# A two-layer decoder step on eight cores: planner waits taken from a table by pair of engines, and up to three seven-product sets open at once

## What is computed

```python
for i in range(DEPTH):                                      # 2 layers
    a = rmsnorm(h, norm_mix[i])
    proj = jnp.einsum('btd,de->bte', a, w_in[i])            # 1024 -> 2048: u, B, C, v
    ...
    y_pool, pb = pool_mixer(u, pool_bufs[i], start, pool_w[i], pool_scale[i])
    z, cb = short_conv(cg * v, conv_bufs[i], conv_w[i], conv_b[i])
    mix = jnp.concatenate([y_pool, bg * z], axis=-1)
    h = h + jnp.einsum('btm,md->btd', mix, w_out[i])
    m = rmsnorm(h, norm_mlp[i])
    f = jax.nn.relu(jnp.einsum('btd,df->btf', m, w_up[i]))  # 1024 -> 4096
    h = h + jnp.einsum('btf,fd->btd', f * f, w_down[i])     # 4096 -> 1024
    gate = jax.nn.sigmoid(jnp.einsum('btd,de->bte', rmsnorm(h, norm_ple[i]), w_ple_gate[i]))
    h = h + gate * jnp.einsum('btq,qd->btd', p[i], w_ple_proj[i])
    ...
return rmsnorm(h, norm_f), ...
```

## Time and profile before

| | us |
|---|---|
| median of 3 runs | 1455.05 (1454.87 to 1456.32) |
| the profiled execution | 1455.05 |
| span of its slowest core (core 1) | 1453.4 |
| spans of the other cores | 1450.8 to 1452.3 |
| mixer of the first layer, up to the first set | 0 to 200.2 |
| MLP of the first layer | 200.2 to about 639 |
| gate of the first, mixer of the second layer | about 639 to 905.5 |
| MLP of the second layer | 905.5 to about 1346 |
| gate and end | about 1346 to 1453.4 |

### The profile page before, as it was taken

One profiled execution on the slowest core, in us unless ns is written; L12 is line 12 of the kernel. 1 busy time (PEld: TensorE's weight loads), 2 busy tenths in 40 slices (PEclk: granted clock), 3 DMA queues, 4 the chain that ended last, 5 costly groups with the idle time before them and its releaser, 6 DMA issues.

```text
span 1453.4 us, 25302 instructions; the slowest of 8 cores (1450.8 to 1453.4 us)
## 1 busy us (share of the span) xinstructions
PE 1404.0 (97%) x7690; PEld 664.8 (46%) x7690; DVE 1261.9 (87%) x2630; ACT 730.5 (50%) x1310; POOL 98.6 (7%) x190
## 2 busy tenths in 40 slices
PE   8999999999999999999999999999999999999995
PEld 5544454344444444443544445444344445444444
DVE  5989899888999877799897998888889988779998
ACT  5553355543553633547534442843554553535766
POOL 3000010000000000100000001100000000000000
PEclk9999999999999999999999999999999999999998
DMA  9900097554444444540050006955554444440124
GB/s 206 222 21 1 1 163 113 88 87 74 87 74 73 74 74 73 87 74 14 11 88 1 1 1 94 150 87 75 86 88 73 74 73 71 75 74 1 22 91 166
DMA packets 31637, 109.23 MB, mean 75 GB/s; under 512 B 3440, under 2 KB 6000, under 8 KB 30704
## 3 DMA queue, kind: packets, MB, share of 16 engines
q0 software_dynamic: 26656, 95.30, 39.1%
q1 hardware_dynamic: 4560, 11.52, 2.2%
q10 hardware_dynamic: 288, 0.79, 0.2%
HBM read 185.38 MB, written 10.10 MB: 134 GB/s over the span
## 4 chain that ended last, share of the span: by engine, by line
PE 84%; DVE 8%; issue 4%; ACT 3%; DMA 0%; DVEq 0%; ACTq 0%
PE ps L435 84%; DVE arena L1005 2%; DVE arena L745 1%; ACT sq L726 1%; DVE sq L714 1%; DVE h L1133 1%; DVE h L1118 1%; DVE arena L1115 1%; DMA h<-x_all 0%; ACT L682 0%; ACT arena L1108 0%; DVE arena L923 0%; ACT ps L945 0%; DVE arena L830 0%; DVE ps L977 0%
## 5 line engine op out<-in xcount | busy, mean ns | idle before, releaser
L435 PE MATMUL ps<-arena,ring 128*128 128x512 bf16 (+4 forms) x5296 | 944.1, 329 | 17.7 <-ACT arena L1108 3.8
L435 PEld LDWEIGHTS ps<-arena,ring 128*128 128x128 bf16 (+1 forms) x5296 | 449.7, 98 | 455.8 <-issue 51.1
L435 PE MATMUL ps<-arena 128*128 128x512 f16 (+3 forms) x2144 | 525.3, 376 | 9.4 <-ACT ps L945 5.6
L435 PEld LDWEIGHTS ps<-arena 128*128 128x128 f16 (+1 forms) x2144 | 194.9, 97 | 294.6 <-issue 107.6
L945 ACT ACTIVATE ps<-ps 128x512 f32<-128x512 f32 x256 | 148.9, 582 | 321.2 <-PE ps L435 275.1
L1020 DVE TENSOR_TENSOR h<-h,ps 128x512 f32<-128x512 f32 x384 | 250.8, 684 | 41.8 <-PE ps L435 35.7
L726 ACT ACTIVATE sq<-h 128x512 bf16<-128x512 f32 x223 | 131.3, 623 | 89.1 <-DVE h L1020 31.4
L745 DVE SCALAR_TENSOR_TENSOR arena<-h,vec,rstd 128x512 bf16<-128x512 f32 (+3 forms) x224 | 143.5, 665 | 2.2 <-ACT rstd L684 2.2
L1001 ACT ACTIVATE arena<-ps 128x512 f32<-128x512 f32 x192 | 113.9, 594 | 61.9 <-PE ps L435 47.2
L923 DVE TENSOR_TENSOR arena<-arena 128x512 f16<-128x512 f16 (+1 forms) x288 | 124.8, 452 | 18.9 <-ACT arena L995 13.9
L938 DVE TENSOR_TENSOR arena<-ring 128x512 f16<-128x512 f16 x256 | 106.9, 420 | 7.1 <-PE ps L435 6.6
(11 more groups left out here) (64 smaller groups left out, 747.0 us busy)
## 6 DMA issues: line engine op xcount, KB each, us to landing
ring<-w_up POOLq DMA_DIRECT2D x64, 512.0 KB, 5.7
ring<-w_down POOLq DMA_DIRECT2D x64, 512.0 KB, 5.7
ring<-w_in POOLq DMA_DIRECT2D x16, 512.0 KB, 9.9
y_all<-h SPq DMA_DIRECT2D x6, 1024.0 KB, 5.6
h<-x_all POOLq DMA_DIRECT2D x4, 1024.0 KB, 45.5
ring<-w_out POOLq DMA_DIRECT2D x8, 512.0 KB, 31.1
ring<-w_gate POOLq DMA_DIRECT2D x8, 512.0 KB, 5.8
h<-x_all POOLq DMA_DIRECT2D x6, 512.0 KB, 19.5
```

Of the source, the lines that this page charges most:

```text
L435: return eng.matmul(self.psum[o.ps.bank][:, o.col:o.col + o.width], lhsT=l, rhs=r, start=(o.fresh and j == 0), stop=(o.last and j == n - 1 ...
```

## The change

The planner's two waits (90 ns behind ACT, DVE and POOL, 190 ns behind PE) become a table by pair of engines, and `AHEAD` goes from 1 to 2. An operation's `end` is now the plain end, and the wait is added where a pair is looked at: in the backward pass, in `make_ready`, in `bank_time` and for the fillers (products without use that keep PE going while the first loads arrive). What is computed, the planner's costs of operations and the rules about banks stay.

```diff
-SEMLAT = 90.0
-PELAT = 190.0
+LAT = {("pe", "act"): 165.0, ("pe", "dve"): 185.0, ("act", "act"): 185.0, ("dve", "dve"): 130.0, ("act", "pe"): 300.0, ("dve", "pe"): 300.0,
+       ("pool", "pe"): 300.0}
+OTHER = 190.0
 DMABW = 315.0
 DMALAT = 2000.0
 WINDOW = 40
-AHEAD = 1
+AHEAD = 2
...
+def lat(d, o):
+
+    return DMALAT if d.chan is not None else LAT.get((d.eng, o.eng), OTHER)
...
         for o in reversed(ops):
-            a = min([s.alap for s in o.succ], default=o.due)
-            a = min(a, o.cap + o.cost + SEMLAT)
-            lat = DMALAT if o.chan is not None else (PELAT if o.eng == "pe" else SEMLAT)
+            a = min([s.alap - lat(o, s) for s in o.succ], default=o.due - OTHER)
+            a = min(a, o.cap + o.cost)
...
-            a -= dur + lat
+            a -= dur
...
                 for n, (_, _, ds) in enumerate(o.mms):
                     for d in ds:
-                        r = max(r, vis[d] - n * o.per)
+                        r = max(r, d.end + (lat(d, o) if d.eng != "pe" else 0.0) - n * o.per)
             else:
-                r = max([vis[d] for d in o.deps], default=0.0)
+                r = max([d.end + lat(d, o) for d in o.deps], default=0.0)
...
-        def bank_time(n):
+        def bank_time(n, e):
...
-            return max(r.end for r in p.readers) + SEMLAT
+            return max(r.end + LAT.get((r.eng, e), OTHER) for r in p.readers)
...
-            o.start, o.end = tau, vis[o]
+            o.start, o.end = tau, end
```

More of the change, by code:

```diff
@@ L258, in schedule @@
         first_set = 0
-        vis = {}
         def make_ready(o):
             if o.mms is not None:
-                r = 0.0 if o.after is None else o.after.end - PELAT
+                r = 0.0 if o.after is None else o.after.end
                 for n, (_, _, ds) in enumerate(o.mms):
                     for d in ds:
-                        r = max(r, vis[d] - n * o.per)
+                        r = max(r, d.end + (lat(d, o) if d.eng != "pe" else 0.0) - n * o.per)
             else:
-                r = max([vis[d] for d in o.deps], default=0.0)
+                r = max([d.end + lat(d, o) for d in o.deps], default=0.0)
             ready[o] = r
@@ L297, in schedule @@
                         pe_first += 1
-                    bt = [(bank_time(n), n) for n in range(8)]
+                    bt = [(bank_time(n, e), n) for n in range(8)]
                     bt = [x for x in bt if x[0] is not None]
@@ L314, in schedule @@
                         f = self.fillers[0]
-                        r = max([free[e], bfree] + [vis.get(d, 1e12) for d in f.deps])
+                        r = max([free[e], bfree] + [1e12 if d.end is None else d.end + lat(d, f) for d in f.deps])
                         if r + f.cost < tau:
@@ L362, in schedule @@
                 end = dma_free
-                vis[o] = end + DMALAT
             elif e == "pe":
-                vis[o] = end + PELAT
                 o.prev = None
@@ L375, in schedule @@
                 pe_done[pe_pos[o]] = True
-            else:
-                vis[o] = end + SEMLAT
-                if o.opens is not None:
-                    o.opens.bank, o.prev = bank, banks[bank]
-                    banks[bank] = o.opens
-            o.start, o.end = tau, vis[o]
+            elif o.opens is not None:
+                o.opens.bank, o.prev = bank, banks[bank]
+                banks[bank] = o.opens
+            o.start, o.end = tau, end
             order[e].append(o)
```

## The result

The changed kernel takes 1400.32 us (median of 4 runs, 1399.75 to 1400.71) against 1455.41 (1454.87 to 1456.32): a ratio of 0.9621, 95% interval 0.9604 to 0.9637. The direction and the mechanism were right; the size was not.

The account below looks back on a forecast made before the run. It took PE as the bound, losing time inside MLP sets to waits for ACT's copies and DVE's add. Gains by groups of quarters, with 0 elsewhere, summed to -33.4 from 1455.05: 1422 us, range 1411 to 1431.

Parts of the forecast that it names:

- The bounds 0.99 and 1.11 us: MLP sets: the copy needs 0.99 us from the end of S2's issue to S3; A22 needs 1.11 behind S3.
- Eight plain quarters: 23.0 lost, 2.4 kept: Plain MLP quarters: PE loses 23.0 us, 2.4 stays for S4's adds in down sets; booked -20.6.
- In their second half DVE already works on the norm ... so I count half: Two quarters before the turn of the token halves: 5.2 us lost, half booked as gain, -2.6.
- the first and last quarters: MLP: two first quarters lose 3.6 us each, booked -3.8; two last lose 2.9 each, booked -4.0; DVE is busy.
- There the wait is DVE's amount of work: Two quarters behind the turn, 60.45 and 62.00 us with DVE busy 59.10 and 59.25: -1.2 each, -2.4.
- I book 0 for it alone: Up to three open sets: only six short places, 128 of 3584 products; the table makes the gain; 0.
- Everything else ... between +2 and -2; 0: Mixer, gate and ends: the row of work is the same but for neighbours; between +2 and -2 us, booked 0.
- the 3 us that the forecast had set as a sign of being wrong: Mixer or gate stages: the forecast called itself wrong if they move by more than 3 us.
- B: Up sets: DVE's full durations count, 6.1 us against PE's 6.05, half the gain; 1438 us, chance 0.13.
- C: PSUM: the eight banks limit, a product put in between finds no free bank; 1455 us, chance 0.04.
- D: A22 of each up set: DVE reaches its add late behind a neighbour set's work; slower, 1489 or 1463 us, chance 0.07.
- A: MLP: every lost microsecond goes, 52.5 us in all; 1403 us, chance 0.06.

Follow-up runs that it names:

- no_dve: The changed kernel with the DVE to PE wait back at the old 90 ns in place of 300: 1419.73 us.
- dve1: The changed kernel with one more 16-bit DVE operation (a repeated subtraction) in each up set, priced zero for the planner: 1407.82 us (0.9673).
- t_ahead1: The changed kernel with its whole table of waits but AHEAD = 1, at most two sets open: 1405.28 us (0.9651).
- act_dve_only: Old waits and AHEAD = 1, only the waits between ACT and DVE, both ways, 190 in place of 90 ns: 1453.96 us beside 1464.36 (0.9923).
- act_pe_only: Old waits and AHEAD = 1, only ACT to PE 300 in place of 90 ns: 1446.31 us against 1464.36 (0.9878).
- dve_pe_only: Old waits and AHEAD = 1, only DVE to PE 300 in place of 90 ns: 1450.32 to 1636.21 us, no verdict.
- act_pe_b: The kernel of act_pe_only run again, unchanged: 1463.75 to 1551.21 us beside a median of 1469.14 before, no verdict.
- dve_pe_b: The kernel of dve_pe_only run again, unchanged: 1471.04 to 1479.16 us beside a median of 1469.14 before, no verdict.
- bank_once: Code of the changed kernel with old waits and AHEAD = 1, leaving only a bank free 90 ns behind its last reader, not 180: 1462.86 us (0.9952).
- after_b: The changed kernel itself, unchanged, run again beside two other kernels: 1400.03 us (0.9568).

## Why the prediction was wrong

- **The mechanism** was right: three waits of PE inside each set, for the copies and for the add, which go once one more product group stands in between. The bounds 0.99 and 1.11 us held: with 1.08 and 1.30 us of products hardly a wait is left. PE's table of waits in after has no row for L1004, and for the copy it has:

```profile
PE ps L434 <- ACT ps L944: 1.5, 2, 0.8
```

- **"Eight plain quarters: 23.0 lost, 2.4 kept"**: hardly anything was kept (the six that stand alone in the table gave 17.0 us of some 17). Six or five products ahead of S4 are enough in the down sets of after. Four are not: the down sets of `no_dve` that have four cost 3.5 us.
- **"In their second half DVE already works on the norm ... so I count half"**, and the same for the first and last quarters: this step failed. It took a DVE that is busy for 86 to 92% of a quarter as one that holds PE up, in the same text that prices an up set by its spacing, 5.5 us of 6.05. Of 5.2 + 5.8 + 7.2 = 18.2 us lost it booked 10.4; all went but some 0.8 us in each first quarter, where S3 of one set still waits for its copy (these two waits). DVE had little room there (0.7 us for four more operations before the turn), but enough.
- **"There the wait is DVE's amount of work"**, at the turn: right that DVE bounds this quarter (`dve1`), wrong in what it bounds it to, and the largest miss inside the MLP, 8.7 us against 2.4. 1.5 of it is the stretch at clock 0.64 of the earlier trace rows, which was left in and whose wait is gone. The table gives 1.5 us per turn beside that (58.92 against 60.45), about the 1.2 that was booked; the third set gives 2.0 more. DVE's 59.10 busy us were no floor: in after three operations fewer than in `t_ahead1` fall into the quarter (123 against 126), and DVE is busy 56.49.
- **"I book 0 for it alone"**, on the third set: the count of places was right (six, 128 of 3584 products), the conclusion wrong. Two of the six are the turns, where PE waited longest, and they hold 4.0 of its 5.0 us. A number of places says nothing on what stands in them.
- **"Everything else ... between +2 and -2; 0"**: it was -6.3, 4.5 of it between the MLPs (0.6 of that a dip of the clock in before's core), past the 3 us that the forecast had set as a sign of being wrong. The products there are the same, but the waits between engines hold there too: `act_dve_only` and `act_pe_only` each take away most of it. The 1.8 of the first mixer and the end were not taken apart.
- **The rivals**: B fell with `dve1` (by full durations it would have cost 27 us, it cost 7.5, a part of it at the turn), C with the plain quarters of 48.46, D with PE's table of waits. A, "every lost microsecond goes", named 1403 with a chance of 0.06, and it is nearly what happened inside the MLP: 48.6 us won there of 52.5. It was put down because of DVE's 59 us behind the turn, which were no floor. The 21.5 us that the sum is short are, by the table above, 6.7 from the three terms that were cut down, 6.3 at the turn (4.0 the third set, 1.5 the clock, 0.8 the table), 6.3 outside the MLP and 2.2 in the plain quarters. So no single term made the range's low end too high: DVE's busy share taken as a bound is behind the 6.7, the third set and the stages outside the MLP put at nothing are behind 4.0 and 6.3, and the slow stretch left in is 1.5.

## What to carry to other kernels

A planner that works in whole products needs not the true wait of each pair but a sum around each loop between engines that lies on the right side of a step: measure the loop in the trace (end of issue to next allowed start), see how many whole products are too short for it, and make the planner's sum larger than those (here 906 ns did as well as 961, with 864 in four products and 990 in the trace's loop). An engine that is busy for nine tenths of a stretch need not bound it; price its work by start-to-start spacing, or add a dummy operation and see whether the time moves. When a rule opens only a few places, look at which places they are before booking it at nothing.

## What the runs showed that was not expected

In two groups of runs (`act_pe_only`, `dve_pe_only`, `act_dve_only`; and `act_pe_b`, `dve_pe_b`, `bank_once`) all cores had a lower mean clock than elsewhere, 0.95 to 0.99 in most executions, and before took 1464 and 1469 us. The expectations above call these stretches half-clock; the rows say otherwise. A window of `act_pe_only`, and its products there and behind it:

```profile
218.00:220.00 2.00, 1.70 (x8) 0.60 (x7) 1.89 (x4) 1.44 (x4) 0.00 (x0) 0.81 1.02 166
```
```profile
218.65 1.21 PE L433 MATMUL ps<-arena 128*128 128x512 f16 x4 [0.30 <-DVE ps L975]
219.68 1.18 PE L433 MATMUL ps<-arena,ring 128*128 128x512 f16 x4
...
221.56 1.89 PE L433 MATMUL ps<-arena,ring 128*128 128x512 f16 x8
223.29 1.03 PE L433 MATMUL ps<-arena 128*128 128x512 f16 x4
```

At 0.81 four products take 1.03 us (218.65 to 219.68), 0.26 each, which is neither of the two levels of 1.2 and 2.4 GHz; from 221.56 eight take 1.73 again. The Trainium skill, TensorE: Matmul & The Clock Gate, section Part 1: The HAM clock gate, names a third state of 13/16 of full speed, 81%, for all-core kernels. These rows agree with the number; the rows of after don't agree that such a kernel must run at it, since its dense plain quarters stand at clock 1.00. On the chip of `act_pe_only` that kernel, which waits less than before, had the lower clock (0.971 to 0.979 against 0.982 to 0.989) and gained 18 us where the copies' waits are 23 to 30. None of the runs of after fell into such a group (`after_b` ran at 0.993 to 0.996, so neither of the guesses on the clock in its expectation was decided), and whether its 55 us hold there is open.
